# Depthwise taps tied to the group behind, with two input buffers; score-decay matmuls in one pack, squares' sum first, the step-size chain one slab sooner

## The chip, the cores and the metric

The kernel runs on one NeuronCore of a Trainium2 chip. The metric is device time in microseconds (us) of one execution; lower is better. The engines named below are TensorE (PE, with its weight loads as PEld), VectorE (DVE), ScalarE (ACT), GpSimd (POOL, which here mostly issues DMAs) and SyncE (SP, which issues the weight loads from HBM).

## The reference, cut to what matters

Two requests of 256 tokens, width 1024, go through two layers. A layer is a gated feed-forward block, a mixer, and a second feed-forward block. The mixer is the part that the change touches:

```python
u = _rms_norm(x, mix_norm[i])
proj = u @ w_in[i]
p_glu, p_z, p_xbc, p_dt, p_gate = jnp.split(proj, splits, axis=-1)
y_a = _conformer_branch(p_glu, ...)   # a * sigmoid(gate), 31-tap depthwise conv, layer norm, silu, matmul
y_b = _ssd_branch(p_z, p_xbc, p_dt, ...)
# in _ssd_branch: 5-tap conv and silu of xbc; dt = softplus(dt_raw + bias); per group of 4 heads, both ways:
#   seg = a_cum[i] - a_cum[j];  decay = exp(where(tril, seg, -inf))
#   y = (scores * decay) @ xdt + states of the other chunk;  y * silu(z), RMS norm over the group
g_a, g_b = jnp.split(jax.nn.sigmoid(p_gate + gate_bias[i]), 2, axis=-1)
x = x + (g_a * y_a + g_b * y_b) @ w_o[i]
```

There are 8 groups of 4 heads. A sequence of 256 is two chunks of 128; the decay matrices of a group are those of a chunk with itself (two chunks, two directions) and those of one chunk with the other (one for each direction).

## The kernel before

All activations lie with features on partitions and the 512 tokens (two requests) on the free axis. Each fp32 product is made as three products of fp32r halves (`three`): weights high by data high, high by low, low by high. A **slab** is 8 such triples, 24 matmuls of 128x512, for 128 output features. Four weight buffers form a ring: SP loads a slab into `wraw`, ACT copies it to `whi`, DVE subtracts to get `wlo` (both are called `split`), and PE runs it. `split` at step t prepares slab t+3.

The mixer of a layer is a sequence of **groups** g = 0 to 9 (`group` on each engine, written out by hand, each engine in its own order). Groups 0 to 7 have 8 steps t, one slab each: gate and a of the convolution, B, C, two slabs of x, two of z. Beside the slabs of group g the engines work on the state-space part of the group behind, H = g - 1 (`ssd`), and on the norm of n = g - 2 (`norm`). Group 8 has the slabs of gate b and the state-space part of group 7; group 9 has the slabs of gate a and the last norm. The names in order of work:

- Step 0, PE: slab 0; scores (line 1461) into banks 4 and 5; eight transposes (line 1469) into banks 2 and 3. ACT: squares of the gated result, silu of the last two conv rows (`conv_silu(H, 2)` and `(H, 3)`), two copies to `zcur`, `split`, tanh of slab 0's bank (line 717, `tg_ready`), then the copies `SC` and `xT`. DVE: taps, `split`.
- Step 1, PE: slab 1, the matmul with ones that sums the squares (line 1477, `gst_ps`), then `seg_diag(0)`: four matmuls of 16 rows (line 1401), one on each quarter of the rows of the array, into banks 2, 3, 6, 7, and the masks for half of the banks, added by PE matmuls (line 1408) where ACT hasn't already written them (line 670). DVE: sum of the squares (line 1122), the input of the depthwise convolution `vp` (line 1142; it waits for slab 1 and sets `v_ready`, which slab 3 waits for).
- Steps 2 and 4, PE: `seg_cross`, two matmuls of 16 rows (line 1416) into banks that a decay has left. ACT: exponentials (`decay`, line 684), masks for the second request. DVE: `both_ways`, norm (line 1150), `scored` at 3 and 5, `gating` at 5 and 7.
- Steps 4 and 6, PE: `y_rows` (line 1425). DVE at steps 4 to 7: the 5-tap convolution of slabs 2 to 5 (`conv_tap_of`, line 1089).

The 31 taps of the depthwise convolution (`unit_tap`, lines 1064 to 1070, DVE) fill the rest of DVE's time. Before, they are one stream over all units: `TAPS_AT` gives the number at each step, 27 in each of groups 1 to 7, 34 in group 8 and 26 in group 9, so that a unit ends in the middle of some group. `vp` has three buffers (`VPS`). The last add of a unit (line 1074) follows its 31st tap, and POOL then writes the unit to `conv_spill`.

In group 0 there is no group behind. Its first two slabs run on data that isn't normalized yet; ACT copies their banks out (line 710, `raw_out`), DVE scales them (lines 1126 to 1133) and ACT takes the tanh between (line 713). Beside it runs the chain `dt_steps`, which makes the step sizes and decay rows: twelve operations on DVE (lines 998 to 1016) at step 2, four transposes on PE (line 1371) at step 4, a product on PE and its split on ACT and DVE at step 5, a second split at 6 and 7. Its results go to DRAM (`r_image`, `l_image`) and come back per group as `RB` and `LB` (`seg_load`, POOL, 8 DMAs), which `seg_diag` waits for (`seg_in`).

Of the kernel before, what the change touches and what calls it, by code (L numbers as in the profile page):

```python
# [21 lines left out]
def trunk(nc, io):  # L22
# [50 lines left out]
    VPS = 3  # L73
# [17 lines left out]
    with ExitStack() as ctx:  # L91
# [82 lines left out]
        with ExitStack() as s3:  # L174
            yz = sb("yz", [P, 2, T], at=s3)
            xpad = sb("xpad", [P, 2, 2, SEQ + TAPS - 1], at=s3)
            zcur = sb("zcur", [P, 2, T], at=s3)
            LB = sb("LB", [P, 2, 2, 2, P], F32R, at=s3)
            cacc = sb("cacc", [P, 2, T], at=s3)
            vp = sb("vp", [P, VPS, 2, SEQ + 2 * HALO], at=s3)  # L180
            cwg = sb("cwg", [P, DWK], at=s3)
# [14 lines left out]
        def operand_of(N):  # L196
# [23 lines left out]
        image_zero, image_set, image_fill, hi_out, lo_out = (  # L220
            sem(n) for n in "image_zero image_set image_fill hi_out lo_out".split())
# [23 lines left out]
        TAPS_AT = [(7, 5, 3, 5, 2, 0, 3, 2)] * (NG - 1) + [(6, 5, 3, 3, 5, 2, 6, 4), (4, 3, 1, 5, 3, 3, 4, 2)]  # L245
        every_tap = iter([(u, k) for u in range(NG) for k in range(DWK)])
        taps_of = [[list(itertools.islice(every_tap, n)) for n in row] for row in TAPS_AT]
        assert next(every_tap, None) is None
        done_at = {u: (i + 1, t) for i, row in enumerate(taps_of) for t, taps in enumerate(row) for u, k in taps if k == DWK - 1}
# [6 lines left out]
        def masks_by(H, r):  # L256

            L, tile = divmod(H, NG)
            return L * (6 * NG - 2) + 6 * tile + 4 * r
# [108 lines left out]
        def _(pool):  # L368
# [23 lines left out]
            def seg_load(L, g):  # L392

                H = L * NG + g
                RB = mixer[L % 2][4]
                need(pool, seg_ps, (H - 1) * EPG)
                for c in range(2):
                    for d in range(2):
                        rows, kinds = seg_rows(c, d), slice(d * KINDS, (d + 1) * KINDS)
                        pool.sem_inc(pool_passed, 1)  # L400
                        pool.dma_start(f32(RB[rows, H % 2, :, :]).rearrange("p r w -> p (r w)"), r_rows[kinds, g, :, c, :]).then_inc(seg_in[H % 2], 16)  # L401
                        pool.dma_start(f32(LB[rows, H % 2, :, :, :]).rearrange("p a r i -> p (a r i)"), l_rows[kinds, g, :, c, :]).then_inc(seg_in[H % 2], 16)

            def conv_spill(L, u):

                U = L * NG + u
                pool.wait_ge(unit_done, U + 1)
                pool.sem_inc(pool_passed, 1)
                pool.dma_start(c_dram[:, u:u + 1].rearrange("r o p t -> p (r o) t"),
                               vp[:, U % VPS, :, HALO:HALO + SEQ]).then_inc(c_out, 16)  # L410

            def group(L, g, norm):

                n = L * NG + g - 2
                for u in range(NG):
                    if done_at[u][0] == g and done_at[u][1] < 2:
                        conv_spill(L, u)
                if 2 <= g < NG:
                    seg_load(L, g)
# [4 lines left out]
                for u in range(NG):  # L424
                    if g <= NG and done_at[u][0] == g and done_at[u][1] >= 2:
                        conv_spill(L, u)

            for L in range(DEPTH):
# [25 lines left out]
                for d in range(2):  # L454
                    pool.wait_ge(q_ready, L * 4 + 3 + d)
                    pool.sem_inc(pool_passed, 1)
                    pool.dma_start(r_diag[d * KINDS + 1], by_pair(qlo, d)).then_inc(lo_out, 16)
                pool.wait_ge(d_lo, L * 2 + 2)
                for d in range(2):
                    pool.sem_inc(pool_passed, 1)  # L460
                    pool.dma_start(l_to(3, d), by_chunk(dlo, d)).then_inc(lo_out, 16)
                    pool.dma_start(x_to(3, d), x_from(dxlo, d)).then_inc(lo_out, 16)
                pool.wait_ge(hi_out, L * 96 + 96)
                pool.wait_ge(lo_out, L * 96 + 96)
                if L == 0:
                    pool.wait_ge(image_set, 16 * 5)
                seg_load(L, 0)
                seg_load(L, 1)
                for g in range(1, NG + 1):
                    group(L, g, g > 1)  # L470
# [3 lines left out]
                for k in range(XT_):  # L474
                    if k == 4:
                        group(L, NG + 1, True)
                    if k == XT_ - 4:
                        conv_spill(L, NG - 1)
# [18 lines left out]
        def _(act):  # L497
# [114 lines left out]
            def dt_steps(L, t):  # L612
# [17 lines left out]
                if t == 5:  # L630
# [11 lines left out]
                    for d in range(2):  # L642
                        a_.dma_start(r_diag[d * KINDS], by_pair(qhi, d)).then_inc(hi_out, 16)
                if t == 6:
# [4 lines left out]
                    for d in range(2):  # L649
                        a_.dma_start(l_to(2, d), by_chunk(dhi, d)).then_inc(hi_out, 16)  # L650
                        a_.dma_start(x_to(2, d), x_from(dxhi, d)).then_inc(hi_out, 16)

            def group(L, g, slabs, ssd, norm, gate=None):
# [19 lines left out]
                def decay(r, e):  # L673
# [8 lines left out]
                    else:  # L682
                        dst, src = M[:, r, e - 4, :, 5 - e, :], bank[2 + 4 * (e - 4)]
                    a_.activation(dst, src[:, :].rearrange("p (h i) -> p h i", h=HPG), ACT.Exp).then_inc(e_ready, 1)

                for t in range(8):
# [19 lines left out]
                    if slabs and not ssd and t < 2:  # L706
                        step(t)
                        if t == 0:
                            need(act, v_ready, G)
                        a_.activation((tg if t == 0 else znew[:, 0])[:, :], bank[t][:, :], ACT.Copy).then_inc(raw_out, 1)  # L710
# [7 lines left out]
                    if t == 0 and ssd:  # L718
# [5 lines left out]
                        for b in range(2):  # L724
                            act.wait_ge(xt_ps, H * 2 + b + 1)
                            a_.activation(xT[:, 2 * b:2 * b + 2, :], bank[2 + b][:, :].rearrange("p (c f) -> p c f", c=2),
                                          ACT.Copy).then_inc(xt_ready, 1)
                    if t == 1 and norm:
                        act.wait_ge(gst_ps, n + 1)
                        need(act, y2_ready, n * 2)  # L730
                        a_.activation(rbc[:, :], bank[4][:, :], ACT.Ln, scale=1.0 / GF, bias=eps_t[:, 0:1]).then_inc(gln, 1)
# [48 lines left out]
                    if slabs and not ssd and t:  # L780
                        dt_steps(L, t)
# [7 lines left out]
            for L in range(DEPTH):  # L789
# [3 lines left out]
                dt_steps(L, 0)  # L793
                for k in range(KD):
# [75 lines left out]
        def _(dve):  # L870
# [173 lines left out]
            def group(L, g, slabs, ssd, norm, gate=False):  # L1044
                G = L * NG + g
                H, n = G - 1, G - 2
                s4 = L * (NSLAB // 4) + g * 2 + S_GROUP // 4
                tg, bc, znew, xT, RB, SC, tn = mixer[L % 2]

                def unit_tap(tile, k):  # L1050

                    U = L * NG + tile
                    src = vp[:, U % VPS, :, k:k + SEQ]
# [18 lines left out]
                    if k == DWK - 1:  # L1072
                        dve.wait_ge(unit_tap_done, U * DWK + DWK)
                        v_.tensor_tensor(vp[:, U % VPS, :, HALO:HALO + SEQ], cacc[:, 0, :].rearrange("p (r t) -> p r t", r=2),
                                         cacc[:, 1, :].rearrange("p (r t) -> p r t", r=2), ALU.add).then_inc(unit_done, 1)
# [42 lines left out]
                for t in range(8):  # L1118
                    if t == 1 and norm:
# [3 lines left out]
                    if t == 2 and slabs and not ssd:  # L1123
# [7 lines left out]
                        need(dve, unit_done, G - VPS + 1)  # L1131
                        dve.wait_ge(c_out, max(G - VPS + 1, 0) * 16 + 16)
                        v_.tensor_tensor(vp[:, G % VPS, :, HALO:HALO + SEQ], tg[:, :].rearrange("p (r t) -> p r t", r=2),
                                         znew[:, 0, :].rearrange("p (r t) -> p r t", r=2), ALU.mult).then_inc(v_ready, 1)
                    if t == 1 and slabs and ssd:
# [4 lines left out]
                        need(dve, unit_done, G - VPS + 1)  # L1140
                        dve.wait_ge(c_out, max(G - VPS + 1, 0) * 16 + 16)
# [431 lines left out]
```

## Time and profile before

| | |
|---|---|
| median of 3 runs | 2914.23 us (2911.5 to 2914.45) |
| the profiled execution | 2910.87 us, its span 2909.1 us |
| PE busy | 2869.3 us, 99% of the span |
| DVE busy | 1867.6 us, 64% |
| ACT busy | 1310.2 us, 45% |
| granted TensorE clock, mean | 0.996 |

The span is cut by the instructions of one execution; what lies around it is 1.8 us. A busy PE means that a matmul was in flight: consecutive matmuls overlap, so that the start of the next, not the duration shown, gives what one costs. The same holds for DVE and ACT, where about 0.1 us of each duration lies under the next one. All shares are means over stages: DVE's busy share is far higher in the mixer's groups than in the feed-forward blocks.

### The profile page before, as it was taken

How to read it: one execution, taken by the hardware profiler on the slowest of the kernel's cores; microseconds unless marked ns; L12 is line 12 of the kernel's file. 1: busy time of each engine (PE TensorE's matmuls, PEld its weight loads, DVE VectorE, ACT ScalarE, POOL GpSimd, SP SyncE). 2: the span in 40 equal slices, each digit the busy share in tenths (PEclk: the TensorE clock that was granted, in tenths of full speed). 3: DMA queues.
4: the chain of work that ended last, by engine and by line, in shares of the span. 5: the costliest groups of instructions: out<-in, count | busy, mean ns of one | idle time of the engine just before them, and what ended most of it. 6: DMA issues, size and time to landing. Idle time of an engine off the chain costs nothing.

```text
span 2909.1 us, 34457 instructions
## 1 busy us (share of the span) xinstructions
PE 2869.3 (99%) x12914; PEld 2315.9 (80%) x12914; DVE 1867.6 (64%) x2387; ACT 1310.2 (45%) x1805; POOL 139.5 (5%) x237
## 2 busy tenths in 40 slices
PE   7999999999999999999999999999999999999998
PEld 5888877777778888888888888777777788888887
DVE  5444479999997654444554436889999866554445
ACT  5322256666664434222342224566676534442223
POOL 1000001110001000000000000100100010000000
PEclk9999999999999999999999999999999999999999
DMA  6333233333335433333333333333333463333332
GB/s 194 97 97 95 81 93 100 106 101 96 104 91 180 110 102 94 96 98 96 94 104 99 94 100 95 91 92 90 103 103 96 116 180 92 95 108 95 101 90 84
DMA packets 532024, 301.88 MB, mean 104 GB/s; under 512 B 17039, under 2 KB 521751, under 8 KB 531895
## 3 DMA queue, kind: packets, MB, share of 16 engines
q1 hardware_dynamic: 511888, 261.65, 31.8%
q0 software_dynamic: 17296, 37.29, 4.3%
q8 instruction: 82, 1.34, 0.2%
q10 hardware_dynamic: 2711, 1.21, 0.2%
q14 instruction: 47, 0.39, 0.0%
HBM read 280.54 MB, written 19.53 MB: 103 GB/s over the span
## 4 chain that ended last, share of the span: by engine, by line
PE 83%; ACT 0%; issue 0%; DMA 0%; POOL 0%; DVE 0%; ACTq 0%
PE bank L1270 78%; PE bank L1425 2%; PE bank L1461 1%; PE bank L1401 0%; PE bank L1416 0%; PE bank L1477 0%; PE bank L1469 0%; PE bank L1408 0%; PE bank L1502 0%; DMA LB<-l_image 0%; ACT hhi L800 0%; PE bank L1305 0%; PE bank L1321 0%; POOL RB L401 0%; ACT o_tm L866 0%
## 5 line engine op out<-in xcount | busy, mean ns | idle before, releaser
L1270 PE MATMUL bank<-uhi,whi 128*128 128x512 f32 x1952 | 767.9, 393 | 13.4 <-DVE ulo L938 11.2
L877 DVE TENSOR_TENSOR wlo<-wraw,whi 128x1024 fp32r<-128x1024 f32 x496 | 605.9, 1223 | 266.8 <-ACT whi L505 256.8
L1270 PE MATMUL bank<-hhi,whi 128*128 128x512 f32 x1952 | 767.9, 393 | 2.2 <-ACT tg L710 2.2
L1270 PE MATMUL bank<-ulo,whi 128*128 128x512 f32 x1952 | 761.0, 390 | 0.0
L1270 PE MATMUL bank<-hlo,whi 128*128 128x512 f32 x1952 | 760.7, 390 | 0.0
L1270 PE MATMUL bank<-hhi,wlo 128*128 128x512 f32 x1952 | 760.5, 390 | 0.0
L1270 PE MATMUL bank<-uhi,wlo 128*128 128x512 f32 x1952 | 760.5, 390 | 0.0
L505 ACT ACTIVATE whi<-wraw 128x1024 fp32r<-128x1024 f32 x496 | 521.5, 1054 | 422.6 <-PE bank L1270 405.7
L1270 PEld LDWEIGHTS bank<-uhi,whi 128*128 128x128 f32 x1952 | 367.0, 188 | 101.3 <-issue 11.7
L1270 PEld LDWEIGHTS bank<-hhi,whi 128*128 128x128 f32 x1952 | 366.8, 188 | 89.8 <-issue 11.7
L1270 PEld LDWEIGHTS bank<-uhi,wlo 128*128 128x128 f32 x1952 | 367.0, 188 | 77.4
L1270 PEld LDWEIGHTS bank<-hhi,wlo 128*128 128x128 f32 x1952 | 366.8, 188 | 77.2
L1270 PEld LDWEIGHTS bank<-ulo,whi 128*128 128x128 f32 x1952 | 367.1, 188 | 75.8 <-issue 1.2
L1270 PEld LDWEIGHTS bank<-hlo,whi 128*128 128x128 f32 x1952 | 366.8, 188 | 75.8 <-issue 1.2
L1070 DVE SCALAR_TENSOR_TENSOR cacc<-vp,cwg,cacc 128x512 f32<-128x512 f32 x464 | 321.8, 746 | 0.0
L1089 DVE SCALAR_TENSOR_TENSOR bc<-xpad,prm,bc 128x512 f32<-128x512 f32 x256 | 191.5, 748 | 3.8
L983 DVE SCALAR_TENSOR_TENSOR xf<-bank,xf 128x512 f32 x64 | 44.3, 692 | 196.1 <-PE bank L1270 196.1
L599 ACT ACTIVATE fa<-fa 128x512 f32<-128x512 f32 x88 | 55.6, 632 | 234.3 <-DVE fa L963 234.3
L966 DVE TENSOR_TENSOR fb<-bank,rbc 128x512 f32<-128x512 f32 x88 | 60.8, 691 | 140.8 <-PE bank L1270 140.8
L750 ACT ACTIVATE bc<-bank,prm 128x512 f32<-128x512 f32 x64 | 49.9, 780 | 183.6 <-DVE bc L1089 144.7
L602 ACT ACTIVATE uhi<-fb 128x512 f32 x44 | 27.8, 632 | 197.8 <-DVE fb L969 197.8
L602 ACT ACTIVATE hhi<-fb 128x512 f32 x44 | 27.8, 632 | 197.7 <-DVE fb L969 197.7
(212 smaller groups left out, 1902.3 us busy)
## 6 DMA issues: line engine op xcount, KB each, us to landing
wraw<-in_ffn_w_up SPq DMA_DIRECT2D x179, 512.0 KB, 3.8
wraw<-in_w_in SPq DMA_DIRECT2D x160, 512.0 KB, 4.0
wraw<-in_ffn_w_down SPq DMA_DIRECT2D x64, 512.0 KB, 3.8
wraw<-in_ssd_w_out SPq DMA_DIRECT2D x32, 512.0 KB, 4.4
wraw<-in_ffn_w_down SPq DMA_DIRECT2D x32, 384.0 KB, 3.3
y_spill<-yz POOLq DMA_DIRECT2D x16, 512.0 KB, 3.3
yraw<-y_spill POOLq DMA_DIRECT2D x32, 256.0 KB, 3.9
wraw<-in_conf_w_out SPq DMA_DIRECT2D x16, 512.0 KB, 4.5
```

Source lines behind the costliest of these rows:

```text
L505: a_.activation(whi[:, t % RING, :], wraw[:, t % RING, :], ACT.Copy).then_inc(hi_ready, 1)
L599: a_.activation(fa[:, j, :], fa[:, j, :], ACT.Silu).then_inc(silu_ready, 1)
L602: a_.activation(h[0][:, bass.ds(i * 2 + j, 1), :], fb[:, j:j + 1, :], ACT.Copy).then_inc(hhi_ready, 1)
L750: a_.activation(bc[:, j, :], bank[t % 2][:, :], ACT.Identity, scale=prm[:, mid:mid + 1], bias=prm[:, P_CB + col:P_CB + col + 1]).then_inc( ...
L877: v_.tensor_tensor(wlo[:, t % RING, :], wraw[:, t % RING, :], f32(whi[:, t % RING, :]), ALU.subtract).then_inc(lo_ready, 1)
L966: v_.tensor_tensor(fb[:, j, :], bank[2 * j + 1][:, :], rbc[:, :], ALU.mult).then_inc(ab_free, 1)
L983: v_.scalar_tensor_tensor(out=xf[:, m, :], in0=bank[4 + q % 2][:, :].unsqueeze(1), scalar=0.5, in1=xf[:, m, :], op0=ALU.mult, op1=ALU.add) ...
L1070: v_.scalar_tensor_tensor(out=dst, in0=src, scalar=cwg[:, k:k + 1], in1=dst, op0=ALU.mult, op1=ALU.add).then_inc(unit_tap_done, 1)
L1089: v_.scalar_tensor_tensor(out=dst, in0=src, scalar=w, in1=dst, op0=ALU.mult, op1=ALU.add).then_inc(cv_ready if k == TAPS - 1 else conv_tap, 1)
L1270: ins = t_.matmul(out, a[:, slot, w], b[:, at + k, :], start=start and k == 0 and a is whi and b is hi, stop=stop and k == nk - 1 and a is ...
L1425: ins = t_.matmul(bank[4 + r][half * HEAD:(half + 1) * HEAD, j * SEQ:(j + 1) * SEQ], xT[:, 2 * r + c, h * HEAD:(h + 1) * HEAD], M[:, r, c, ...
L1461: ins = t_.matmul(bank[4 + r][:, c * SEQ:(c + 1) * SEQ], bc[:, 0, chunk(2 * r + c)], bc[:, 1, request(r)], start=True, stop=True)
```

## The change

1. **Taps.** Group g runs the 31 taps of unit g - 1, in `TAP_SLICES` of 8, 6, 4, 5, 2, 0, 4 and 2; group 9 has none. The last add moves to the end of step 7. `vp` has two buffers, so `vp` of group g waits until unit g - 2 is in DRAM.
2. **Packs.** `seg_cross` goes: its two matmuls follow the four of `seg_diag` and write banks 4 and 5. Six exponentials follow at once, at steps 1 and 3. ACT writes the masks of all four banks for the first request too (two more, line 670, at step 0), except in the first group of a layer, where PE still adds four. `y_rows(0)` now waits for all twelve exponentials.
3. **Squares' sum.** DVE adds the squares at the start of step 0, and PE's matmul with ones comes at the end of step 0, into bank 0; for that it waits until the tanh has read bank 0 (`tg_ready`).
4. **The step-size chain** is called with t + 1: its DVE part comes at step 1, ahead of DVE's `split` of slab 4 and ahead of the scaling at step 2, the transposes after slab 3, the product after slab 4, and so on. ACT copies slab 0's bank ahead of the eight copies of line 800. The loads of `RB` go out before the low halves are written, those of `LB` after; each waits for its own writes only.

```diff
-        TAPS_AT = [(7, 5, 3, 5, 2, 0, 3, 2)] * (NG - 1) + [(6, 5, 3, 3, 5, 2, 6, 4), (4, 3, 1, 5, 3, 3, 4, 2)]
+        TAP_SLICES = [(0, 8), (8, 14), (14, 18), (18, 23), (23, 25), (25, 25), (25, 29), (29, DWK)]
@@ POOL
-                seg_load(L, 0)
-                seg_load(L, 1)
+                pool.wait_ge(qhi_out, L * 32 + 32)
+                pool.wait_ge(qlo_out, L * 32 + 32)
+                r_load(L, 0)
+                r_load(L, 1)
                 pool.wait_ge(d_lo, L * 2 + 2)
...
+                pool.wait_ge(dhi_out, L * 64 + 64)
+                pool.wait_ge(dlo_out, L * 64 + 64)
+                l_load(L, 0)
+                l_load(L, 1)
@@ ACT
+                        if H % NG:
+                            act.wait_ge(xt_ready, H * 2 + 2)
+                            for d in range(2):
+                                mask(0, d)
...
-                        for e in range(4):
+                        for e in range(EPR):
                             decay(t // 2, e)
-                    if ssd and t in (2, 4):
-                        for e in range(4, EPR):
-                            decay(t // 2 - 1, e)
...
-                        dt_steps(L, t)
+                        dt_steps(L, t + 1)
...
+                act.wait_ge(slab_done, L * NSLAB + S_GROUP + 1 + RING)
+                need(act, v_ready, L * NG)
+                a_.activation(mixer[L % 2][0][:, :], bank[0][:, :], ACT.Copy).then_inc(raw_out, 1)
                 for k in range(KD):
@@ DVE
-                    if t == 1 and norm:
+                    if t == 0 and norm:
                         dve.wait_ge(gsq, n * 2 + 2)
...
-                        dve.wait_ge(c_out, max(G - VPS + 1, 0) * 16 + 16)
+                        dve.wait_ge(c_out, max(G - 1, 0) * 16 + 16)
...
-                    if slabs and not ssd and 0 < t < 7:
-                        dt_steps(L, t)
+                    if slabs and not ssd and 0 < t < 6:
+                        dt_steps(L, t + 1)
                     if slabs or gate:
                         split(s4 + t // 4, t % 4)
...
+                    if t == 7 and ssd:
+                        dve.wait_ge(unit_tap_done, U * DWK + DWK)
+                        v_.tensor_tensor(vp[:, U % 2, :, HALO:HALO + SEQ], cacc[:, 0, :].rearrange("p (r t) -> p r t", r=2),
@@ PE
-                    by_act = 2 if r else 1 if H % NG else 0
+                    by_act = r or H % NG
...
-                        t_.matmul(bank[2 + 4 * c][:, :], LB[rows, H % 2, 1, r, :], RB[rows, H % 2, r, :], start=True, stop=True).then_inc(seg_ps, 1)
+                        ins = t_.matmul(bank[4 + c][:, :], LB[rows, H % 2, 1, r, :], RB[rows, H % 2, r, :], start=True, stop=True)
...
+                        if t == 2 and norm and ssd:
+                            pe.wait_ge(gln, n + 1)
...
-                    if t == 1 and norm:
+                    if t == (0 if ssd else 1) and norm:
                         pe.wait_ge(gsq_sum, n + 1)
                         if ssd:
-                            pe.wait_ge(sc_ready, H * 2 + 1)
-                        t_.matmul(bank[4][:, :], ones[:, :], sq[:, 0, :], start=True, stop=True).then_inc(gst_ps, 1)
+                            pe.wait_ge(*((tg_ready, G + 1) if slabs else (gate_ready, L * 2 * KD + gate + 1)))
+                        t_.matmul(bank[0 if ssd else 4][:, :], ones[:, :], sq[:, 0, :], start=True, stop=True).then_inc(gst_ps, 1)
...
-                        seg_cross(1)
-                        if norm:
-                            pe.wait_ge(gln, n + 1)
-                        pe.wait_ge(sc_ready, H * 2 + 2)
+                        pe.wait_ge(e_ready, H * EPG + EPG)
                         y_rows(0)
```

## Rows read from the trace of the kernel before

**Rows 1.** The page's busy times: us, share of the span, instructions.

```profile
PE 2869.3 (99%) x12914; PEld 2315.9 (80%) x12914; DVE 1867.6 (64%) x2387; ACT 1310.2 (45%) x1805; POOL 139.5 (5%) x237
```

**Rows 2.** PE's waits in the whole span: total us, times, longest.

```profile
PE bank L1270 <- ACT tg L710: 4.4, 2, 2.2
PE bank L1401 <- issue: 2.7, 1, 2.7
PE bank L1401 <- DMA LB<-l_image: 1.1, 1, 1.1
```

**Rows 3.** Timeline of PE in group 4, first layer: start us, us, operation.

```profile
623.03 1.02 PE L1477 MATMUL bank<-sq,ones 128*128 128x512 f32 x2
623.98 0.51 PE L1401 MATMUL bank<-RB,LB 16*128 16x512 f32 x4
624.41 0.73 PE L1408 MATMUL bank<-never,identr 128*128 128x512 f32 x2
624.98 0.39 PE L1270 MATMUL bank<-uhi,whi 128*128 128x512 f32 x1
...
630.22 0.39 PE L1270 MATMUL bank<-uhi,wlo 128*128 128x512 f32 x1
630.54 0.50 PE L1416 MATMUL bank<-RB,LB 16*128 16x512 f32 x2
630.97 0.50 PE L1270 MATMUL bank<-uhi,whi 128*128 128x512 f32 x1
```

**Rows 4.** Timeline of DVE in the same group, with idle time and its releaser.

```profile
614.65 4.72 DVE L1070 SCALAR_TENSOR_TENSOR cacc<-vp,cwg,cacc 128x512 f32<-128x512 f32 x7
...
623.22 0.69 DVE L1142 SCALAR_TENSOR_TENSOR vp<-tg,bank 128x512 f32<-128x512 f32 x1 [2.11 <-PE bank L1270]
...
627.26 0.69 DVE L1074 TENSOR_TENSOR vp<-cacc 128x512 f32<-128x512 f32 x1
627.87 1.22 DVE L877 TENSOR_TENSOR wlo<-wraw,whi 128x1024 fp32r<-128x1024 f32 x1
...
648.61 2.36 DVE L1106 TENSOR_TENSOR M<-M,SC 128x1024 f32<-128x1024 f32 x2 [0.93 <-ACT M L684]
...
667.71 1.22 DVE L877 TENSOR_TENSOR wlo<-wraw,whi 128x1024 fp32r<-128x1024 f32 x1
```

**Rows 5.** DVE's write of vp three groups later: durations, first and last start.

```profile
L1142 DVE SCALAR_TENSOR_TENSOR vp<-tg,bank x1: 691/691/691, 785.6 to 785.6; 128x512 f32<-128x512 f32 x1
```

**Rows 6.** Timeline of ACT at step 0 of group 4.

```profile
613.63 0.63 ACT L666 ACTIVATE bc<-bc 128x512 f32<-128x512 f32 x1 [1.26 <-DVE bc L1089]
...
616.16 0.58 ACT L717 ACTIVATE tg<-bank 128x512 f32<-128x512 f32 x1
```

**Rows 7.** Timelines of PE, DVE and ACT in group 0, first layer.

```profile
410.77 0.50 PE L1270 MATMUL bank<-uhi,whi 128*128 128x512 f32 x1 [2.21 <-ACT tg L710]
...
427.36 0.46 PE L1371 MATMUL bank<-ident,dtf 64*128 64x64 f32 x4
```

```profile
410.26 1.23 DVE L877 TENSOR_TENSOR wlo<-wraw,whi 128x1024 fp32r<-128x1024 f32 x1 [0.25 <-ACT whi L505]
...
414.23 0.69 DVE L1128 SCALAR_TENSOR_TENSOR tg<-tg,rbc 128x512 f32<-128x512 f32 x1 [0.70 <-ACT tg L713]
...
415.56 0.41 DVE L998 TENSOR_SCALAR du<-de 64x512 f32<-64x512 f32 x1
...
423.79 2.35 DVE L877 TENSOR_TENSOR wlo<-wraw,whi 128x1024 fp32r<-128x1024 f32 x2
```

```profile
416.58 0.78 ACT L750 ACTIVATE bc<-bank,prm 128x512 f32<-128x512 f32 x1 [2.39 <-PE bank L1270]
417.26 0.59 ACT L752 ACTIVATE xpad<-bank 128x512 f32<-128x512 f32 x1
```

**Rows 8.** Window after PE's 2.7 us wait, second layer: us, busy times, PEclk.

```profile
1893.65:1897.28 3.63, 3.63 (x11) 2.81 (x9) 3.57 (x6) 2.55 (x5) 0.00 (x0) 0.53 0.33 87
```

**Rows 9.** DMA issues by kind: count, KB each, median us to landing.

```profile
conv_spill<-vp POOLq DMA_DIRECT2D x16, 256.0 KB, 2.7
```

More of the change, by code:

```diff
@@ L398, in seg_load, with l_load, group @@
                     for d in range(2):
-                        rows, kinds = seg_rows(c, d), slice(d * KINDS, (d + 1) * KINDS)
                         pool.sem_inc(pool_passed, 1)
[L401 to L417, printed above, removed]
+                        pool.dma_start(f32(RB[seg_rows(c, d), H % 2, :, :]).rearrange("p r w -> p (r w)"),
+                                       r_rows[d * KINDS:(d + 1) * KINDS, g, :, c, :]).then_inc(seg_in[H % 2], 16)
+            def l_load(L, g):
+                H = L * NG + g
+                for c in range(2):
+                    for d in range(2):
+                        pool.sem_inc(pool_passed, 1)
+                        pool.dma_start(f32(LB[seg_rows(c, d), H % 2, :, :, :]).rearrange("p a r i -> p (a r i)"),
+                                       l_rows[d * KINDS:(d + 1) * KINDS, g, :, c, :]).then_inc(seg_in[H % 2], 16)
+            def group(L, g, ssd, norm):
+                G = L * NG + g
+                U, n = G - 1, G - 2
                 if 2 <= g < NG:
-                    seg_load(L, g)
+                    r_load(L, g)
+                    l_load(L, g)
                 if norm:
@@ L423, in group @@
                     pool.dma_start(y_dram[g * 2 - 4:g * 2 - 2].rearrange("k p t -> p k t"), yz[:, :, :]).then_inc(y_out, 16)
-                for u in range(NG):
-                    if g <= NG and done_at[u][0] == g and done_at[u][1] >= 2:
-                        conv_spill(L, u)
+                if ssd:
+                    pool.wait_ge(unit_done, U + 1)
+                    pool.sem_inc(pool_passed, 1)
+                    pool.dma_start(c_dram[:, g - 1:g].rearrange("r o p t -> p (r o) t"),
+                                   vp[:, U % 2, :, HALO:HALO + SEQ]).then_inc(c_out, 16)
             for L in range(DEPTH):
@@ L475, in _ @@
                     if k == 4:
[L476 to L478 removed]
+                        group(L, NG + 1, False, True)
                     if k == XT_ - 2:
@@ L705, in group @@
                         gate(t)
-                    if slabs and not ssd and t < 2:
+                    if slabs and not ssd and t == 1:
                         step(t)
-                        if t == 0:
-                            need(act, v_ready, G)
-                        a_.activation((tg if t == 0 else znew[:, 0])[:, :], bank[t][:, :], ACT.Copy).then_inc(raw_out, 1)
+                        a_.activation(znew[:, 0, :], bank[1][:, :], ACT.Copy).then_inc(raw_out, 1)
                     if slabs and not ssd and t == 2:
@@ L727, in group @@
                                           ACT.Copy).then_inc(xt_ready, 1)
+                        if H % NG:
+                            act.wait_ge(xt_ready, H * 2 + 2)
+                            for d in range(2):
+                                mask(0, d)
                     if t == 1 and norm:
@@ L730, in group @@
                         need(act, y2_ready, n * 2)
-                        a_.activation(rbc[:, :], bank[4][:, :], ACT.Ln, scale=1.0 / GF, bias=eps_t[:, 0:1]).then_inc(gln, 1)
+                        a_.activation(rbc[:, :], bank[0 if ssd else 4][:, :], ACT.Ln, scale=1.0 / GF, bias=eps_t[:, 0:1]).then_inc(gln, 1)
                         act.wait_ge(gln, n + 1)
@@ L1155, in group @@
                         gating(t // 2 - 2)
-                    if slabs and not ssd and t == 7:
-                        dt_steps(L, t)
-                    taps = taps_of[g - 1][t] if g else []
+                    if slabs and not ssd and t == 6:
+                        dt_steps(L, t + 1)
+                    taps = range(*TAP_SLICES[t]) if ssd else ()
                     for k in range(max(len(taps), TAPS)):
```

94 lines of the change are left out of this document (42 added, 52 removed).

## The prediction

> **What bounds the kernel now.** I read the page's busy times first: TensorE is busy for 99% of the span, so only its work and its waits count [rows 1]. Then PE's waits: in the mixer there are two waits of 2.2 us for the copy of slab 0's bank in group 0, and one of 2.7 and one of 1.1 us ahead of the first `seg_diag` of a layer [rows 2]. So there is little waiting to remove; what a group costs is its PE work. Then the timelines of one group with a group behind. From one write of `vp` to the one three groups later the trace has 785.6 - 623.22 = 162.4 us, 54.13 us for a group [rows 4, 5]. In that time DVE is idle for only 2.11 us, where it waits for slab 1, and 0.93 us, where it waits for an exponential [rows 4]. DVE is thus 3.0 us short of being the bound in the twelve groups 2 to 7 of both layers. That nearness decides the case: the change takes work from PE and gives DVE more.
>
> **What PE saves.** A matmul in a slab starts 0.23 us after the last one. A separate cross pack is entered after 630.54 - 630.22 = 0.32 us, 0.09 more; it takes 630.97 - 630.54 = 0.43 us; and the first matmul behind it shows 0.50 us where others show 0.39, 0.11 more: 0.63 us in all [rows 3]. The pack of four diagonals takes the same 0.43 us (623.98 to 624.41), so matmuls on different quarters of the rows run together [rows 3]. The two crosses use two quarters that the diagonals already hold, so joined they cost another pass, 0.22 us; the bounds are 0 and 0.43 us. At step 2 the joining saves 0.63 - 0.22 = 0.41. At step 4 `y_rows` follows directly, so entry and exit stay and 0.43 - 0.22 = 0.21 is saved; 0.62 for a group. The two mask matmuls take 624.98 - 624.41 = 0.57 us, less the exit of 0.11 that the pack then pays: 0.46, in seven groups of a layer [rows 3]. For two layers that is 2 x (8 x 0.62 + 7 x 0.46) = 16.4 us of PE work. The matmul with ones only moves: 0.95 us (623.03 to 623.98) either way [rows 3]. The two masks and the early exponentials are ACT's, which is busy 45% of the time [rows 1]; they lie under slabs 1 and 4. If that cover were gone, they would cost PE two ACT operations, about 1.2 us by the sizes of the ACT rows [rows 6, 7].
>
> **What the taps cost.** A group has 31 taps where it had 27. Seven taps take 4.72 us, 0.67 each [rows 4], so DVE gets 4 x 0.67 = 2.7 us more, against 3.0 us of idle time and a PE period that shrinks by 0.62 + 0.46 = 1.08 us to 53.05. That would be a tie but for the order of things. The moved matmul with ones waits for the tanh of slab 0's bank, which stands on ACT behind the silu of the last conv row, behind two copies and a `split`; that silu waits for DVE's last conv tap at step 7. So a ring closes once per group, and I walk it:
> - Slab 1's end to the start of `vp`: 623.22 - 623.03 = 0.19 us [rows 3, 4].
> - `vp` to the end of step 7's conv taps on DVE: now 667.71 - 623.22 = 44.49 us. The idle 0.93 goes, because the exponentials come earlier (before, they stood behind an ACT copy that waited for DVE). The last add, 627.87 - 627.26 = 0.61, moves behind the conv taps. Steps 1 to 7 get 23 taps for 20, 2.01 us. So 44.49 - 0.93 - 0.61 + 2.01 = 44.96, and 0.09 until the last of them ends [rows 4].
> - ACT from silu to the end of the tanh: 616.16 + 0.58 - 613.63 = 3.11 us [rows 6].
> - The handover to PE, 0.05; the matmul with ones, 0.95; slab 1, 630.54 - 624.98 = 5.56 us [rows 3].
>
> The ring takes 54.91 us, 0.78 more than 54.13. PE has only 53.05 us of work in it, so it waits 1.86 us in each period, nearly all ahead of the matmul with ones. Group 2 is spared: the period ahead of it has no norm on DVE and more masks on PE. Groups 3 to 8 remain: 12 x 0.78 = +9.3 us. Outside these periods the saving comes through: 0.62 in group 1 and 1.08 in group 8, -3.4 us for two layers. What else is queued behind the waiting matmul is PE's slab 1, and behind it `vp`, which is in the ring. Without ring and lag, the same periods would bring 12 x -1.08.
>
> **What group 0 costs.** The early copy of slab 0's bank removes PE's 2.21 us wait: slab 2 starts at 408.56 instead of 410.77 [rows 7], and slab 3 ends 2 x 5.56 later, at 419.7. But DVE's twelve operations, 423.79 - 415.56 = 8.23 us, now stand ahead of its `split` of slab 4 and of the scaling. `split` of slab 3 ends at 410.26 + 1.23 = 411.5; the chain at 419.7; the next `split` at 420.9; scaling and tanh, 0.69 + 0.70, at 422.3; ACT's two copies of slab 2's bank, 417.26 + 0.59 - 416.58 = 1.27, at 423.5 [rows 7]. They stand behind the tanh on ACT and slab 4 waits for them. The transposes (about 0.4) end at 420.1, so PE waits 3.4 us. Before, slab 4 started at 410.77 + 11.1 = 421.9, with the transposes still to come: a loss of 1.6 - 0.4 = 1.2 us. To this comes the clock. After the 2.7 us wait in the second layer the granted clock was 0.53 for 3.63 us, the lower of the two levels, 1.2 instead of 2.4 GHz, which costs 3.63 x 0.47 = 1.7 us; I take the same for the 3.4 us here [rows 2, 8]. That makes 2.9 us a layer, +5.8; bounds -2.2 (the old wait gone, no new one) and +5 (ACT's DMA issues, now ahead of the silu of z, add a wait too). The Trainium skill, "TensorE: Matmul & The Clock Gate", section on the reasons why this matters for kernels, says that idle gaps between bursts of matmuls put the clock back to its lower level; by that rule the 1.7 us are paid here too, while without it the sum would be 3.4 us lower. The trace agrees for the gap of 2.7 us and shows no fall behind the one of 2.2.
>
> **What the earlier loads save.** The waits of 1.1 and 2.7 us for `LB` and `RB` go, since the rows are split about 3 us sooner and `RB` no longer waits for the low halves; with the clock's 1.7 us that is -5.5 us [rows 2, 8]. On POOL's queue the eight `RB` issues pass ahead of the low halves' writes, which are not ready sooner anyway.
>
> **The two buffers** cost nothing: from a unit's last add to the next `vp` DVE has the squares' sum, eight taps and a `split`, 7 us, and about 1.3 us of waiting; the spill lands 2.7 us after its issue of 0.7 [rows 9], so 4.8 us are left.
>
> **Sum:** 9.3 - 3.4 + 5.8 - 5.5 = +6.2 us. On the profiled execution's 2910.87 us that is 2917.1. The median of the runs shown is 3.4 us above that execution, so I forecast 2920.4 us, 0.2% above the median of before. Changes within 0.2%, 5.8 us, are about what a measurement of this kernel can't tell from none.
>
> **Rivals.** *PE stays the bound.* If the ring is shorter than PE's 53.05 us, by 1.86 us or more, all savings come through: -13.0 - 3.4 + 5.8 - 5.5 = -16.1 us, 2898. For it speaks that DVE's summed work is only about 53.8 us; against it that this is already above 53.05. Chance 0.15. *It cancels.* The ring is 0.3 us shorter (each 0.1 is 1.2 us) and group 0 costs about 2 us less in total: near 2915. Chance 0.15. *The clock falls at the recurring waits.* The ones wait of nearly 1.9 us comes twelve times; if each brought the 1.7 us of rows 8, the time were 12 x 1.7 = 20 us more, 2941. Against it: the 2.2 us waits brought no fall. Chance 0.12. *The spill makes `vp` wait.* It decides from a landing of about 7.5 us, and each us above costs 12 us; 0.03. The forecast's own case has 0.55 with its own range 2912 to 2930: 0.5 us of ring either way is 6 us, group 0's bounds the rest. Of it I put 0.33 above +0.2%, since a wait that I overlooked only adds, 0.20 within and 0.02 below. So slower 0.33 + 0.12 + 0.03 = 0.48, same 0.20 + 0.12 = 0.32, faster 0.15 + 0.03 + 0.02 = 0.20. The range of 2897 to 2936 takes in the first two rivals and leaves out the falls of the clock and the spill.
>
> **What would show it.** Right: PE waits of 1.5 to 1.9 us ahead of the matmul with ones, released by ACT's tanh, in groups 3 to 8; a period of 54.9 us between writes of `vp`; DVE idle about 1.3 us ahead of `vp`; a wait of about 3.4 us ahead of slab 4 in group 0; none ahead of `seg_diag`. Wrong: periods near 53.1 us and no PE waits (the first rival), the granted clock under 0.9 in groups 3 to 8 (the third), or DVE waiting on a DMA at `vp`.

## The result and the profile after

| | before | after |
|---|---|---|
| median | 2914.13 us (7 runs, 2911.5 to 2915.45) | 2922.44 us (7 runs, 2921.91 to 2924.42) |
| ratio to before | | 1.0033, 95% interval 1.0023 to 1.0042 |
| profiled execution | 2910.87 us, span 2909.1 | 2922.44 us, span 2920.7 |

The changed kernel is slower by 8.3 us, 0.3%. The two spans differ by 11.6 us, because the profiled execution of before ran 3.3 us under its median and that of after on its median; what is compared between traces below adds up to about that. The trace of a single execution also holds how often and how long the clock fell in it; the last section says by how much that varies.

The page of the changed kernel, its busy times (us, share, instructions), beside [rows 1]:

```profile
PE 2863.0 (98%) x12886; PEld 2311.7 (79%) x12886; DVE 1864.4 (64%) x2387; ACT 1330.1 (46%) x1837; POOL 140.5 (5%) x237
```

PE has 28 matmuls less and 6.3 us less busy time, and the span is longer all the same. (The change also writes the eight transposes of line 1469 as matmuls with a transpose flag; that costs nothing: from their first start to slab 1 pass 0.80 us before and 0.79 in e4, where slab 1 follows them directly too.) Its waits say why, beside [rows 2]:

```profile
PE bank L1478 <- ACT tg L713: 9.7, 10, 1.0
...
PE bank L1270 <- ACT xpad L752: 6.5, 3, 3.0
PE bank L1270 <- issue: 4.3, 2, 2.2
PE bank L1478 <- ACT mix L808: 2.2, 2, 1.1
PE bank L1270 <- ACT znew L774: 1.0, 2, 0.5
```

Line 1478 is the matmul with ones: it waits twelve times, ten for the tanh of slab 0's bank and two, in group 8, for the tanh of gate b (`mix`). The waits ahead of `seg_diag` and the 2.2 us for slab 0's bank are gone. New are 3.0 us in each group 0, 2.2 us in each group 8 with no releaser named, and small ones.

The ring of a group, on the timelines of the changed kernel (PE, then DVE, then ACT; start us, us, operation, idle time before). They answer to [rows 3, 4, 6]:

```profile
621.02 1.10 PE L1478 MATMUL bank<-sq,ones 128*128 128x512 f32 x2 [0.98 <-ACT tg L713]
621.56 0.80 PE L1270 MATMUL bank<-uhi,whi 128*128 128x512 f32 x1
627.51 0.50 PE L1401 MATMUL bank<-RB,LB 16*128 16x512 f32 x4
...
628.18 0.50 PE L1270 MATMUL bank<-uhi,whi 128*128 128x512 f32 x1
...
675.79 1.10 PE L1478 MATMUL bank<-sq,ones 128*128 128x512 f32 x2 [0.74 <-ACT tg L713]
...
682.31 0.50 PE L1401 MATMUL bank<-RB,LB 16*128 16x512 f32 x4
```

```profile
627.62 0.69 DVE L1138 SCALAR_TENSOR_TENSOR vp<-tg,bank 128x512 f32<-128x512 f32 x1 [1.35 <-PE bank L1270]
...
672.42 1.22 DVE L877 TENSOR_TENSOR wlo<-wraw,whi 128x1024 fp32r<-128x1024 f32 x1
673.56 0.69 DVE L1170 TENSOR_TENSOR vp<-cacc 128x512 f32<-128x512 f32 x1
674.16 0.69 DVE L1118 TENSOR_TENSOR sq<-sq 128x512 f32<-128x512 f32 x1
...
682.42 0.69 DVE L1138 SCALAR_TENSOR_TENSOR vp<-tg,bank 128x512 f32<-128x512 f32 x1 [1.38 <-PE bank L1270]
```

```profile
672.54 0.63 ACT L664 ACTIVATE bc<-bc 128x512 f32<-128x512 f32 x1 [2.43 <-DVE bc L1085]
673.08 1.13 ACT L698 ACTIVATE zcur<-znew 128x512 f32<-128x512 f32 x2
674.12 1.04 ACT L503 ACTIVATE whi<-wraw 128x1024 fp32r<-128x1024 f32 x1
675.07 0.58 ACT L713 ACTIVATE tg<-bank 128x512 f32<-128x512 f32 x1
```

Follow it: `vp` starts at 627.62; DVE works without a gap until its `split` behind the last conv tap (672.42, after 44.80 us); ACT takes silu, two copies, `split` and tanh, 672.54 to 675.65 (675.07 + 0.58); the matmul with ones starts at 675.79; slab 1 ends at 682.31, and `vp` starts at 682.42. The period is 54.80 us (before: 54.13), and every piece is within 0.2 us of the one that was forecast. The joined pack takes 628.18 - 627.51 = 0.67 us.

Group 0 of the first layer (PE's timeline; the first row is a matmul with ones ahead of the mixer's slabs, the fourth the sixth matmul of slab 4), and the window of the slow matmuls (us, busy times of PE, PEld, DVE, ACT, POOL, granted clock, share of the DMA engines, GB/s), beside [rows 7, 8]:

```profile
394.37 1.02 PE L1305 MATMUL bank<-acc,ones 128*128 128x512 f32 x2
...
419.66 0.43 PE L1371 MATMUL bank<-ident,dtf 64*128 64x64 f32 x4 [0.42 <-DVE dtf L1016]
423.12 0.79 PE L1270 MATMUL bank<-uhi,whi 128*128 128x512 f32 x1 [3.03 <-ACT xpad L752]
...
425.42 0.63 PE L1270 MATMUL bank<-uhi,wlo 128*128 128x512 f32 x1
...
455.93 1.89 PE L1461 MATMUL bank<-bc 128*128 128x256 f32 x8
```

```profile
423.12:428.80 5.68, 5.68 (x14) 4.48 (x15) 4.12 (x6) 5.19 (x7) 0.00 (x0) 0.52 0.60 157
```

PE waits 3.03 us; after it the granted clock is 0.52 for 5.68 us, the lower level, and matmuls start 0.43 us apart in place of 0.23. The scores of group 1 start at 455.93 us, where before they started at 451.74: 4.2 us lost (forecast: 2.9). Counted from the matmul of line 1305, which started at 394.57 before, it is 61.56 us against 57.17, 4.4 us; in the second layer 61.62 against 57.13, 4.5 us.

Group 8, PE and ACT:

```profile
846.67 0.50 PE L1401 MATMUL bank<-RB,LB 16*128 16x512 f32 x4
847.01 0.39 PE L1407 MATMUL bank<-RB,LB 16*128 16x512 f32 x2
849.56 0.47 PE L1270 MATMUL bank<-uhi,whi 128*128 128x512 f32 x1 [2.16 <-issue]
```

```profile
846.78 0.69 ACT L808 ACTIVATE mix<-bank,hbias 128x512 f32<-128x512 f32 x1 [2.64 <-PE bank L1270]
847.48 1.28 ACT L731 ACT_TABLE_LOAD   x1
848.78 0.69 ACT L731 ACTIVATE rbc<-bank,eps_t 128x512 f32<-128x512 f32 x1
```

Slab 2 waits for the logarithm that reads the squares' sum out of bank 0, and that ends at 849.47. It stands on ACT behind the tanh of slab 1's bank (which waits for slab 1) and a table load. The profile names no releaser; experiment e5 does.

### The profile page after: what moved, and what is told of

The parts are those of the page before. It is cut to its first block, busy times and chain, and to the rows that moved or that the text cites. A ratio compares the mean times of both kernels' runs of the same rounds, so it can differ in the third digit from the quotient of the medians.

```text
span 2920.7 us, 34511 instructions
## 1 busy us (share of the span) xinstructions
PE 2863.0 (98%) x12886; PEld 2311.7 (79%) x12886; DVE 1864.4 (64%) x2387; ACT 1330.1 (46%) x1837; POOL 140.5 (5%) x237
## 3 DMA queue, kind: packets, MB, share of 16 engines
q10 hardware_dynamic: 2711, 1.21, 0.2%
## 4 chain that ended last, share of the span: by engine, by line
PE 78%; DVE 17%; issue 3%; ACT 2%; DMA 0%; ACTq 0%; DVEq 0%; SPq 0%
PE bank L1270 75%; DVE cacc L1070 5%; DVE bc L1085 4%; DVE wlo L877 3%; DVE M L1102 2%; DVE M L1093 1%; PE bank L1478 1%; DVE yz L1146 1%; PE bank L1423 1%; DVE yz L1110 0%; PE bank L1461 0%; PE bank L1499 0%; ACT zcur L698 0%; DVE vp L1138 0%; DMA x_tm<-in_x_sample 0%
```

## The experiments

All but e8 and e10 edit the changed kernel. Times are medians; the interval is that of the ratio to the kernel before, which was measured again beside each group of experiments (2912.9 to 2914.1 us). The changed kernel was not, so differences to its 2922.4 us are good to about 1 us. A diff shows the lines that matter; "..." marks what is left out.

**e1, two taps moved from step 4 to step 0.**

```diff
-TAP_SLICES = [(0, 8), (8, 14), (14, 18), (18, 23), (23, 25), (25, 25), (25, 29), (29, DWK)]
+TAP_SLICES = [(0, 10), (10, 16), (16, 20), (20, 25), (25, 25), (25, 25), (25, 29), (29, DWK)]
```

> The changed kernel with two taps moved from step 4 to step 0 (slices of 10, 6, 4, 5, 0, 0, 4, 2). The ring (write of vp, DVE to the last conv tap of step 7, ACT's silu to tanh, the matmul with ones, slab 1) loses 1.1 us, so the period goes from 54.8 to about 53.75 us and the kernel from 2922.4 to about 2910; the PE waits ahead of the matmul with ones shrink. Rival, DVE's summed work is the bound: no tap is removed, so the time stays at 2922 and the period at 54.8.

2910.41 us (0.9978 to 0.9997). The period is 732.59 - 678.88 = 53.71 us, and DVE has no idle time ahead of `vp`:

```profile
678.88 0.69 DVE L1138 SCALAR_TENSOR_TENSOR vp<-tg,bank 128x512 f32<-128x512 f32 x1
...
732.59 0.69 DVE L1138 SCALAR_TENSOR_TENSOR vp<-tg,bank 128x512 f32<-128x512 f32 x1
```

No work was removed, yet 12 us went (12 x (54.77 - 53.71) = 12.7 by the periods; 54.77 us is the changed kernel's mean period). The rival falls: where the taps stand sets the time, not their number.

**e2, two taps moved the other way.**

```diff
-TAP_SLICES = [(0, 8), (8, 14), (14, 18), (18, 23), (23, 25), (25, 25), (25, 29), (29, DWK)]
+TAP_SLICES = [(0, 6), (6, 12), (12, 16), (16, 21), (21, 25), (25, 25), (25, 29), (29, DWK)]
```

> The same with two taps moved the other way, from step 0 to step 4 (slices of 6, 6, 4, 5, 4, 0, 4, 2). The ring theory: 1.26 us more in the ring, period about 56.05 us, 12 x 1.26 = 15 us more, 2937; DVE idles 2.6 us ahead of vp. Rival, DVE's summed work: no change, 2922.

2940.4 us (1.0073 to 1.0107), 18 us more than the changed kernel; DVE idles 2.69 us ahead of `vp`, and the period is 742.96 - 686.97 = 55.99 us:

```profile
686.97 0.69 DVE L1138 SCALAR_TENSOR_TENSOR vp<-tg,bank 128x512 f32<-128x512 f32 x1 [2.69 <-PE bank L1270]
...
742.96 0.69 DVE L1138 SCALAR_TENSOR_TENSOR vp<-tg,bank 128x512 f32<-128x512 f32 x1 [2.70 <-PE bank L1270]
```

The twelve periods give 12 x 1.21 = 14.5 us, as expected. The 3 us above the expectation lie outside them: the ring now binds in group 2 too (its matmul with ones waits 0.53 us in each layer), and the clock fell in both groups 8, which took 1.6 us more each.

**e3, the tanh ahead of the copies and `split`.**

```diff
                             conv_silu(H, 3)
 
+                            step(0)
+                            if gate:
+                                gate(0)
+                            else:
+                                need(act, v_ready, G)
+                                a_.activation(tg[:, :], bank[0][:, :], ACT.Tanh, scale=0.5).then_inc(tg_ready, 1)
                             act.wait_ge(z_ready, H * 2 + 4)
...
-                    if gate:
+                    if gate and not (ssd and t == 0):
...
-                    if ssd and slabs and t == 0:
-                        step(0)
-                        need(act, v_ready, G)
-                        a_.activation(tg[:, :], bank[0][:, :], ACT.Tanh, scale=0.5).then_inc(tg_ready, 1)
```

> The changed kernel with ACT's tanh of slab 0's bank (in group 8 that of gate b) right behind the silu, ahead of the two copies to zcur and of split. That takes 2.1 us out of the ring, to about 52.7 us; DVE's own work of 53.5 us is then the bound and its idle time ahead of vp goes: 12 x 1.3 = 16 us less, 2906. Rival, the period is set by the conv taps and exponentials at steps 4 to 6 (the waits for xpad): no change, 2922.

2915.28 us (0.9995 to 1.0014): 7 us less, not 16. The timelines of DVE, ACT and PE show why:

```profile
671.94 0.68 DVE L1120 TENSOR_TENSOR sq<-sq 128x512 f32<-128x512 f32 x1
...
679.33 0.69 DVE L1140 SCALAR_TENSOR_TENSOR vp<-tg,bank 128x512 f32<-128x512 f32 x1 [0.51 <-PE bank L1272]
...
733.26 0.69 DVE L1140 SCALAR_TENSOR_TENSOR vp<-tg,bank 128x512 f32<-128x512 f32 x1 [0.52 <-PE bank L1272]
```

```profile
670.86 0.58 ACT L700 ACTIVATE tg<-bank 128x512 f32<-128x512 f32 x1
```

```profile
672.68 1.12 PE L1480 MATMUL bank<-sq,ones 128*128 128x512 f32 x2
```

The tanh ends at 671.44 now (670.86 + 0.58), but the matmul with ones starts at 672.68, right behind DVE's sum of the squares (671.94 + 0.68 = 672.62), which stands behind `split` and the last add on DVE. A second way round the same ring, only 0.8 us shorter: the period is 53.93 us. My expectation had overlooked it. The periods alone would give 12 x 0.84 = 10 us; why the median shows only 7 is not traced.

**e4, the matmul with ones back at step 1, still into bank 0.**

```diff
-                    if t == (0 if ssd else 1) and norm:
+                    if t == 1 and norm:
                         pe.wait_ge(gsq_sum, n + 1)
```

> The changed kernel with the matmul with ones back at step 1, after slab 1, still into bank 0 (DVE's sum stays at step 0). The ring through the tanh is then gone; what is left through the silu, the transposes and slab 1 is about 52 us, so DVE's work of 53.5 us binds: 12 x 1.3 = 16 us less, 2906. Against it a wait of slab 2 for the logarithm, a few tenths of a us in a group and up to 2.5 us more in group 8. Rival, the order of the sum is free: 2922.

2901.03 us (0.994 to 0.9973), 21 us less. No PE wait stands ahead of line 1478 any more, slab 2 waits 0.16 us, and the period is 729.69 - 676.35 = 53.34 us with DVE never idle ahead of `vp`:

```profile
676.35 0.69 DVE L1138 SCALAR_TENSOR_TENSOR vp<-tg,bank 128x512 f32<-128x512 f32 x1
...
729.69 0.68 DVE L1138 SCALAR_TENSOR_TENSOR vp<-tg,bank 128x512 f32<-128x512 f32 x1
```

12 x (54.77 - 53.34) = 17 us come from the periods; in group 8 PE's longest wait without a releaser is 1.3 us in place of 2.2, 2 us for both layers. One condition of the change cost more than its net loss.

**e5, the logarithm first in group 8.**

```diff
                         split(s4 + t // 4, t % 4)
+                    if t == 1 and norm and gate and ssd:
+                        act.wait_ge(gst_ps, n + 1)
...
+                        a_.activation(rbc[:, :], rbc[:, :], ACT.Exp, scale=-0.5).then_inc(gr_ready, 1)
                     if gate:
                         step(t)
                         gate(t)
...
-                    if t == 1 and norm:
+                    if t == 1 and norm and not (gate and ssd):
```

> The changed kernel; only in group 8 ACT takes the logarithm and the root of the squares' sum ahead of the tanh of slab 1's bank, where it stood behind it and a table load. If slab 2 of group 8 waits there for the logarithm (2.16 us in each layer, released by nothing that the profile names), both waits go: about 4.3 us less, 2918. Rival, it waits for its weights or for the tanh: no change or more, 2922.

2916.59 us (1.0003 to 1.0022), 5.9 us less than the changed kernel (5.0 if both are taken against the kernel before measured beside them); both 2.16 us waits are gone from PE's list. The logarithm was the releaser.

**e6, the step-size chain at step t again.**

```diff
-                        dt_steps(L, t + 1)
+                        dt_steps(L, t)
```

on ACT, DVE and PE, with DVE's steps 0 < t < 7 behind the taps and step 7 ahead of them, as before the change.

> The changed kernel with the step-size chain called at step t again on DVE, ACT and PE; the early copy of slab 0's bank and the split loads stay. My theory: the 3.0 us wait ahead of slab 4 of group 0 and the fall of the clock behind it go, and group 0 ends 2.2 us earlier than before the change, about 6.4 us a layer: 2910. The loads of LB are still in time. Rival, the chain's shift pays by the loads: the waits of 1.1 and 2.7 us ahead of seg_diag come back and the time stays near 2920.

2909.5 us (0.9979 to 0.9997), 12.9 us less. Group 1's scores start at 448.62 us, 7.3 before the changed kernel and 3.1 before the old one, and PE has no wait in group 0 and none ahead of `seg_diag`: the split loads and the early copy together bring that without the shift (which of the two, no run separates).

```profile
424.24 0.46 PE L1371 MATMUL bank<-ident,dtf 64*128 64x64 f32 x4
...
448.62 1.89 PE L1461 MATMUL bank<-bc 128*128 128x256 f32 x8
```

**e7, PE adds all masks of the first request.**

```diff
-                    by_act = r or H % NG
+                    by_act = r
```

and ACT's `mask(0, d)` at step 0 and `mask(1, d)` at step 5 left out, with the count of masks that PE waits for adapted.

> The changed kernel with all four masks of the first request added by PE in every group, and ACT's four masks for them left out: four more matmuls of 0.28 us on PE in groups 2 to 8, 1.1 us a group. The ring theory: PE has 1.7 us of waiting in each of the 12 periods, so only groups 2 and 8 pay: 2 to 5 us more, 2925 to 2927. Rival, PE's work sets the time: 14 x 1.1 = 16 us more, 2938.

2921.03 us (1.0016 to 1.0038): no more than the changed kernel, with 56 matmuls more on PE. Its waits shrink instead. Those ahead of the matmul with ones go from 9.7 us to 6.5 for ten (PE's waits):

```profile
PE bank L1469 <- ACT tg L713: 6.5, 10, 0.7
```

The wait ahead of slab 7 (0.41 us at 661.27 in the changed kernel) is gone, and in group 8 the masks lie under the wait for the logarithm, 1.05 us in place of 2.16. In the changed kernel PE's work is not what sets the time in these groups; what it was relieved of became waiting.

**e8, the kernel before with part 1 alone.**

```diff
-        TAPS_AT = [(7, 5, 3, 5, 2, 0, 3, 2)] * (NG - 1) + [(6, 5, 3, 3, 5, 2, 6, 4), (4, 3, 1, 5, 3, 3, 4, 2)]
+        TAPS_AT = [(8, 6, 4, 5, 2, 0, 4, 2)] * NG + [(0,) * 8]
...
-    VPS = 3
+    VPS = 2
```

> The kernel before with part 1 of the change alone: 31 taps of the unit behind in each of groups 1 to 8, none in group 9, two buffers. With the matmul with ones at step 1 no ring runs through the tanh, and DVE's work, 53.4 us a group, stays under PE's 54.13: no change, 2911 to 2915, DVE's idle time ahead of vp small. Rival, the taps by themselves delay PE: 12 x 0.7 = 8 us more, 2922.

2917.51 us (1.001 to 1.0028), 4.7 us above the kernel before measured beside it: between the two expectations. The period is 732.27 - 677.65 = 54.6 us, and DVE has one idle stretch in it:

```profile
649.32 2.36 DVE L1104 TENSOR_TENSOR M<-M,SC 128x1024 f32<-128x1024 f32 x2 [0.92 <-ACT M L682]
```

```profile
677.65 0.69 DVE L1140 SCALAR_TENSOR_TENSOR vp<-tg,bank 128x512 f32<-128x512 f32 x1
...
732.27 0.69 DVE L1140 SCALAR_TENSOR_TENSOR vp<-tg,bank 128x512 f32<-128x512 f32 x1
```

With the old packs the wait for the exponential of [rows 4], 0.93 us, stays, and DVE has no other idle time in the period: its work, 53.7 us, and this wait make the 54.6, above PE's 54.13. My expectation had counted DVE's work as if the packs were joined.

**e10, the kernel before with part 3 alone** (DVE's sum at step 0, the matmul with ones at the end of step 0 into bank 0, the wait for the logarithm ahead of slab 2):

```diff
-                    if t == 1 and norm:
+                    if t == (0 if ssd else 1) and norm:
                         pe.wait_ge(gsq_sum, n + 1)
                         if ssd:
-                            pe.wait_ge(sc_ready, H * 2 + 1)
-                        t_.matmul(bank[4][:, :], ones[:, :], sq[:, 0, :], start=True, stop=True).then_inc(gst_ps, 1)
+                            pe.wait_ge(*((tg_ready, G + 1) if slabs else (gate_ready, L * 2 * KD + gate + 1)))
+                        t_.matmul(bank[0 if ssd else 4][:, :], ones[:, :], sq[:, 0, :], start=True, stop=True).then_inc(gst_ps, 1)
```

> The kernel before with part 3 alone: DVE's sum of the squares at the start of step 0, the matmul with ones at its end into bank 0. The ring then exists with the old taps: 0.11 + 44.49 + 0.12 + 3.11 + 0.14 + 6.5 = 54.5 us against PE's 54.13, 12 x 0.35 = 4 us, and slab 2 of group 8 waits 2.2 us for the logarithm in each layer: 8 us more, 2921 to 2922. Rival, the order of the sum costs only together with the taps: 2914.

2919.08 us (1.0014 to 1.0035), 6.2 us above. The period is (786.86 - 569.24) / 4 = 54.4 us, and slab 2 of group 8 waits 1.73 us. The rows are ACT's tanh and PE's matmul with ones of group 4, then slab 2 of group 8:

```profile
616.32 0.57 ACT L717 ACTIVATE tg<-bank 128x512 f32<-128x512 f32 x1
```

```profile
617.03 1.10 PE L1479 MATMUL bank<-sq,ones 128*128 128x512 f32 x2
...
844.45 0.47 PE L1270 MATMUL bank<-uhi,whi 128*128 128x512 f32 x1 [1.73 <-issue]
```

The matmul with ones starts 0.14 us after the tanh ends (616.89), the same handover as in the changed kernel, while DVE idles 2.4 us ahead of `vp`. So the ring binds with the old taps too; 12 x 0.27 = 3 us from it and 2 x 1.73 us in group 8 make the 6.2. The part costs by itself.

**e9, what the experiments point to:** e4, e5 and e6 together.

> The changed kernel with the matmul with ones at step 1, the step-size chain at step t, and the logarithm first in group 8. If the three causes are separate, their gains add: 21.4 from the sum at step 1, 12.8 from the chain, 2 to 3 from the logarithm: 2885 to 2887. Rival, they share the same waits: 2895 or more.

2885.6 us (0.9892 to 0.9923), 27.6 us below the kernel before measured beside it and 37 below the changed one. The three causes add: 21.4 (e4), 12.9 (e6) and 2.6 for what e4 leaves of the two waits for the logarithm (2 x 1.3) are 36.9. Its last waits in the groups are 0.2 us:

```profile
PE bank L1276 <- issue: 2.2, 14, 0.2
```

**e11, e9 with the stream of taps and three buffers of before** (`TAPS_AT`, with 27 taps in groups 1 to 7, 34 in group 8 and 25 in group 9, `VPS = 3` and `conv_spill` as they stood).

> The combined kernel with the taps as the stream of before (27 in a group, three buffers). There DVE's work, 53.34 us, is the bound of a group; with four taps less PE's 53.05 us binds: 12 x 0.3 = 3.5 us less, 2882. Rival, DVE isn't the bound there: no change, 2885.6.

2886.54 us (0.9899 to 0.9929): no gain. The period is 53.21 us against e9's 53.33, and DVE idles 2.2 us ahead of `vp`: PE binds, at 53.2 and not at 53.05, so at most 1.4 us were to be had. The difference is no work: PE still waits 0.16 us ahead of slab 2 for the logarithm, 14 times here as in e9. Once packs are joined and the ring is open, the tied taps and two buffers cost nothing that can be measured.

```profile
669.63 0.69 DVE L1163 SCALAR_TENSOR_TENSOR vp<-tg,bank 128x512 f32<-128x512 f32 x1 [2.22 <-PE bank L1291]
722.85 0.69 DVE L1163 SCALAR_TENSOR_TENSOR vp<-tg,bank 128x512 f32<-128x512 f32 x1 [2.20 <-PE bank L1291]
```

## Why the prediction was right, and where its sizes were off

- **The ring (+9.3 us forecast)** was right in mechanism, place and nearly in size: the mean period is 54.77 us against 54.91 forecast. e1 and e2 show it by moving taps across it, e4 by opening it. 12 x (54.77 - 54.13) = 7.7 us. That PE would wait 1.5 to 1.9 us ahead of the matmul with ones was too much: it waits 0.7 to 1.1 there, and the rest of its 1.6 us sits in front of slabs 6 and 7, which wait for ACT's copies of banks behind DVE's conv taps (0.41 us ahead of slab 7 at 661.27).
- **PE's savings (16.4 us)** were there as work: the joined pack takes 0.67 us against 0.65 forecast, and where nothing but PE binds (e11) a group takes 53.21 us with a wait of 0.16 in it, 53.05 of work as forecast. (The 6.3 us less of busy time don't measure it: the slow matmuls of group 0 count as busy.) But in twelve periods they turned into waiting, as forecast; e7 shows it by giving the masks' part back for nothing. In e9, where they come through up to DVE's own work, the period is 53.33.
- **Group 0 (+5.8 us)** is a term of the sum that was mis-sized: 4.4 and 4.5 us, 8.9 in all between the two traces. The wait came as walked, 3.03 + 0.42 us against 3.4. The clock's part was too small: I took the 3.63 us of [rows 8], here the clock was at the lower level for 5.68 us, which costs 5.68 x 0.48 = 2.7 us, not 1.7. Part of that is the chance of one execution: over the 14 such waits in the traces of the changed kernel, e1 to e5 and e7 the slow matmuls last 2.7 to 5.7 us, 4.2 in the mean, about 2.1 us lost; with them a group 0 takes 61.1 us in the mean, against 57.7 in the six of the kernel before, e8 and e10: 3.4 us a layer. And ACT's DMA issues delayed the silu of z: PE waits 0.5 us for it in each layer (`znew`), which I had only in the bounds. e6 shows that the place of the chain causes the term: with it at step t a group 0 takes 54.6 us in both layers, and 2 x (61.1 - 54.6) = 13 us is what its median gained.
- **The loads (-5.5 us)** were right in that no wait is left ahead of `seg_diag`. The reason given was too narrow: e6 shows that the split loads and the early copy do it without the shift of the chain.
- **Group 8** is the term that was missing. I named the new wait of slab 2 for the logarithm only in the quoted diff and never walked it. In groups 2 to 7 it is hidden; in group 8 ACT's tanh of slab 1's bank stands ahead of the logarithm: 2.16 us a layer, 4.3 in all, shown by e5. It cost more than its length: in 4 of 10 such waits (changed kernel, e1, e2, e3, e6) the clock fell behind it, at 1.6 us each.
- **The sum:** 6.2 - 1.6 for the ring + 3.1 for group 0 + 4.3 for group 8 = 12.0 us, against 11.6 between the spans. So between the traces the terms were off by more than 5 us. By medians the change costs 8.3 us, since the profiled execution of before ran 3.3 us low, and that the forecast of 2920.4 came within 2.0 us of the median is in part luck: the low execution covers most of the missing term. What made it low is known in part only. In the second layer its wait of 2.2 us for slab 0's bank brought no fall of the clock; in e8's and e10's traces it did, at 1.6 us.
- **The rivals.** PE as the bound is out (e7). The clock didn't fall at the recurring waits: the granted clock is 1.00 in the stretch of groups 1 to 7 (the window's columns as above), and no trace has slow matmuls there. The argument against it, that waits of 2.2 us bring no fall, came from one trace and doesn't hold (last section). DVE never waited for a DMA at `vp`; three buffers gain nothing (e11).

```profile
455.00:840.00 385.00, 378.09 (x1801) 291.25 (x1799) 370.41 (x510) 258.92 (x404) 39.52 (x65) 1.00 0.35 96
```

e5 gave 5.9 us where its two waits are 4.3. The spans of the two traces differ by 5.5 us: 2.2 us in each group 8, and 1.1 us in group 0 of the second layer, where the slow matmuls behind the 3.0 us wait last 3.1 us in place of 5.3. In the median the falls of the clock behind the waits of group 8 go too; by the 4 in 10 above they are worth 0.4 x 2 x 1.6 = 1.3 us, an estimate. What stays open: 3 us of e3, and the rest of the 3.3 us by which the profiled execution of before ran low.

## What to carry to other kernels

Before a step is moved ahead, walk the ring that it closes: from the operation that waits, through every engine's queue in order, back to itself. Here a matmul that was moved 6 us earlier tied TensorE to the end of VectorE's and ScalarE's queues and cost more than 16 us of saved matmul work brought in. And when an engine is relieved, look at how near the next one is: packing saves TensorE 1.1 us of 54.1 in a group, but with the ring open (e4, e9) the period falls by 0.8 only, to the 53.3 us of VectorE's own work.

## What the hardware showed that I had not expected

Apart from the clock the thirteen traces repeat closely: from group 9 of the first layer to the mixer of the second (the matmul with ones of either) they take 932.97 to 933.01 us. The falls of the clock don't repeat. Three windows of slow matmuls, of e1 (group 8), e8 and e3 (group 0), in the columns used above:

```profile
843.69:846.68 2.99, 2.99 (x8) 2.30 (x7) 2.06 (x3) 2.98 (x7) 0.00 (x0) 0.50 0.14 16
```

```profile
1842.90:1845.88 2.98, 2.98 (x8) 2.32 (x7) 2.08 (x4) 2.26 (x4) 0.00 (x0) 0.50 0.59 157
```

```profile
423.66:426.39 2.73, 2.73 (x7) 2.17 (x8) 1.38 (x2) 2.72 (x3) 0.00 (x0) 0.50 0.40 112
```

The start of the kernel left aside, the traces show this:

- All 14 waits of 3.03 us were followed by the lower level, for 2.7 to 5.7 us, and so were the waits of 2.7 and 2.8 us in the kernel before and in e8. A wait of 3 us, in a kernel that is otherwise 98% busy, cost 1.4 to 2.9 us more than its length (half of the time at the lower level).
- Of the 17 waits of 2.2 us (2.16 to 2.21), 7 were followed by it, at about 1.6 us each; the same wait of the same kernel brings it in one layer and not in the other (e1: the first layer, not the second).
- No wait of 1.73 us or less was followed by it, the recurring ones of about 1 us (1.2 in e2) included.

So one trace in which a wait of 2.2 us costs only its length does not show that it always does.
